# A hybrid decoder step on one core: meta rows and sequences in one chunk, the last input blocks between the chunks' steps, and one convolution tap on ScalarE

## The reference

```python
h = h + W_out(concat[GDN(xn), Conformer(xn)])      # xn = RMSNorm(h), one projection W_in for both
h = h + PEER(RMSNorm(h))                           # 128*128 experts of one neuron, 8 heads, top 16
y = RMSNorm(h)
# GDN: 4 heads of 128; q, k, v through a causal convolution of 4 taps and silu, q and k normalised
#   per chunk: decay = exp(G_i - G_j), L = strict(k beta k^T decay), solve (I + L) u = [v beta, k beta exp(G)]
#   v_new = u_v - w_k S;  o = (q exp(G)) S + (q k^T decay) v_new
#   S = S exp(G_last) + (k exp(G_last - G))^T v_new
#   prompt: one chunk of 16 meta rows, then chunks of 64; sequences: the recurrence, 4 steps each
# Conformer: glu = a * sigmoid(b); causal convolution of 31 taps over 512 channels; LayerNorm; silu
```

## Time and profile before

| | |
|---|---|
| median of 3 runs (us) | 1945.18 |
| lowest and highest (us) | 1933.81, 1945.46 |
| the profiled execution's own time (us) | 1947.19 |
| its span, first to last instruction (us) | 1945.5 |
| mean granted TensorE clock in it | 0.963 |

### The profile page before, as it was taken

The page is one execution under the profiler, slowest core; times in us unless marked ns, Lnnn a source line. Parts: engine busy times, 40 slices in busy tenths (PEclk is TensorE's granted clock), DMA queues, the critical chain, the costliest instruction groups (busy, mean ns, idle before and its releaser), DMA issues.

```text
span 1945.5 us, 29596 instructions
## 1 busy us (share of the span) xinstructions
PE 1819.2 (94%) x11654; PEld 1761.5 (91%) x11654; DVE 1432.6 (74%) x2619; ACT 659.0 (34%) x1046; POOL 668.3 (34%) x431
## 2 busy tenths in 40 slices
PE   5999676887989999999999999999999999999998
PEld 4999566765989999999999999999999999999997
DVE  4798788556359999999986666635878877888753
ACT  4444211112143334434343333333333333333332
POOL 2000000000000067767787676773324333333100
PEclk9999798875989999999999999999999999999999
DMA  7321100000552148798989999899999999999831
GB/s 192 88 66 53 50 1 1 1 1 19 163 168 85 45 153 280 257 310 286 324 295 311 301 312 313 304 318 374 350 356 384 356 348 341 367 341 339 326 122 36
DMA packets 190859, 424.86 MB, mean 218 GB/s; under 512 B 11188, under 2 KB 119248, under 8 KB 180473
## 3 DMA queue, kind: packets, MB, share of 16 engines
q1 hardware_dynamic: 153409, 287.99, 42.9%
q0 software_dynamic: 37312, 134.97, 19.5%
HBM read 361.28 MB, written 62.06 MB: 218 GB/s over the span
## 4 chain that ended last, share of the span: by engine, by line
PE 73%; DVE 22%; issue 2%; ACT 1%; DMA 1%; POOL 1%; SPq 0%; DVEq 0%; ACTq 0%; POOLq 0%
PE psum L1160 30%; PE psum L1139 20%; PE psum L829 9%; PE psum L1127 3%; PE psum L824 3%; PE psum L917 2%; DVE junk L2047 2%; DVE cT L1624 2%; DVE besti L1910 1%; DVE sring L1914 1%; DVE besti L1922 1%; PE psum L975 1%; DVE best L1918 1%; DVE best L1906 1%; DVE WR L1541 1%
## 5 line engine op out<-in xcount | busy, mean ns | idle before, releaser
L1139 PE MATMUL psum<-xT,WS 128*128 128x416 f32 x3072 | 594.7, 353 | 2.9 <-POOL WS L766 2.9
L1160 PE MATMUL psum<-AR,WS 128*128 128x416 f32 x3072 | 582.1, 351 | 2.6 <-DVE AR L2118 2.6
L1160 PEld LDWEIGHTS psum<-AR,WS 128*128 128x128 f32 x3072 | 575.6, 188 | 9.1 <-DVE AR L2118 3.0
L1139 PEld LDWEIGHTS psum<-xT,WS 128*128 128x128 f32 x3072 | 572.1, 188 | 8.5 <-POOL WS L766 4.1
L766 POOL TENSOR_TENSOR WS<-RAWP,WS 128x1024 fp32r<-128x1024 f32 x128 | 311.7, 2445 | 773.5 <-ACT WS L1441 673.0
L757 POOL DMA_INDIRECT rowg<-in_expert_v,idx x128 | 176.9, 1382 | 322.6 <-DVE acc L2061 315.1
L829 PE MATMUL psum<-xT,WR 128*128 128x280 f32 (+1 forms) x1968 | 261.1, 295 | 2.6 <-DVE xT L1567 2.6
L829 PEld LDWEIGHTS psum<-xT,WR 128*128 128x128 f32 x1968 | 258.2, 193 | 3.3 <-DVE xT L1567 3.2
L1451 ACT ACTIVATE WS<-RAWP 128x1024 fp32r<-128x1024 f32 x128 | 135.6, 1059 | 337.8 <-PE psum L1160 337.8
L2111 DVE TENSOR_TENSOR WS<-RAWP,WS 128x1024 fp32r<-128x1024 f32 x128 | 156.4, 1222 | 116.7 <-ACT WS L1451 116.7
L1478 ACT ACTIVATE actA<-psum 128x416 f32<-128x416 f32 x128 | 66.4, 519 | 402.9 <-PE psum L1139 402.7
(11 more groups left out here) (334 smaller groups left out, 1668.0 us busy)
## 6 DMA issues: line engine op xcount, KB each, us to landing
RAWP<-in_expert_u SPq DMA_DIRECT2D x64, 1024.0 KB, 6.3
RAWP<-in_expert_v SPq DMA_DIRECT2D x64, 1024.0 KB, 8.6
act_dram<-actA SPq DMA_DIRECT2D x128, 208.0 KB, 4.4
gate_dram<-gblk SPq DMA_DIRECT2D x26, 1024.0 KB, 10.5
act<-act_dram SPq DMA_DIRECT2D x64, 416.0 KB, 8.2
Gt<-gate_dram SPq DMA_DIRECT2D x16, 1664.0 KB, 9.7
RAW<-in_w_in SPq DMA_DIRECT2D x8, 1024.0 KB, 5.6
RAW<-in_w_query SPq DMA_DIRECT2D x8, 1024.0 KB, 5.6
```

What stands on the lines that cost most here:

```text
L1139: last = mm(bank[e % 2][:, 0:TD], ws(e)[:, pw, kt * P:(kt + 1) * P], xT[:, px, kt, TSP:TPE], start=(kt == 0 and i == 0), stop=(kt == KT - ...
L1160: last = mm(bank[dt][:, 0:TD], ws(NK + e)[:, pw, dt * P:(dt + 1) * P], AR[:, e % 4, pa, :], start=(e == 0 and i == 0), stop=(e == NK - 1 a ...
```

## The change

The 32 rows of the sequences and the 16 meta rows become one chunk of 48, chunk 0, and stand first in the rows, so that five chunks are left. Masks (`tri_m`, `neg_m`, `pos_m`) keep the sequences apart. The input blocks are put in the order ab, glu 0, qkv, glu 1, glu 3, glu 2, z 0, z 1. The last five of them (from `LATE`) are no longer a stretch of their own: their units, cut in halves of 12 products, are steps of the same written order as the chunks' steps. That order is now given by a level for each step. The sets of tiles are three. Each group of products waits for the readers of its bank's last group, in a ring of four banks while input blocks run, of six after. Exponentials get their bias on ScalarE, per head; the scalings of k and v and the decay of the state move from VectorE to ScalarE, per head; the copies of the tail rows too. The factor of q is left to the output's norm. The LayerNorm is computed with channels on partitions, its sums by products with ones. The sequences' states are updated within the stretch. The sums of q's and k's squares move to the last four qkv blocks, and the wait for `qk2` stays ahead of the interleaved part. The first tap of each qkv convolution is done by ScalarE after the unit is taken out. SyncE's loads (states, `h`, the rows of the norm, weights with other slots) are reordered accordingly.

```diff
-CHUNKS = [(0, 128), (128, 128), (256, 128), (384, 128), (512, 16), (TP, TS)]
-SAMPLE = len(CHUNKS) - 1
+MIXED = TS + META
+CHUNKS = [(0, MIXED)] + [(MIXED + P * i, P) for i in range(SEQ // P)]
...
-    blocks += [glu[1], z[0], z[1], glu[3], glu[2]]
+    blocks += [glu[1], glu[3], glu[2], z[0], z[1]]
...
+LATE = 8
...
+        SET = {0: 0, 1: 0, 2: 0, 3: 1, 4: 2}
+        FIRST = {0: 4.2, 1: 13.5, 2: 30.5, 3: 40.3, 4: 43.3}
+
+        LEVEL = {"k": 0, "gb": 0.1, "khT": 1, "kk": 2, "kq": 2.1, "ldT": 3, "v": 3.1, "p2": 4, "pt2": 4.1,
+                 "t1": 5, "p4": 5.1, "pt4": 5.2, "t2": 6, "p8": 6.1, "t3": 7, "n": 8, "nt": 8.1, "r0a": 8.2,
+                 "r0b": 8.3, "n2": 9, "r1a": 9.1, "r1b": 9.2, "nt2": 9.3, "nt4": 10, "r2a": 10.1, "r2b": 10.2,
+                 "r3a": 11, "r3b": 11.1, "wT": 12, "ws": 13, "qs": 13.1, "su": 14, "o1": 14.1}
...
+        SAMPLE_AT = {"sw0": 46.4, "sw1": 47.4, "sw2": 48.4, "sw3": 49.4, "sw": 49.5, "ws": 50.4, "qs": 50.5,
+                     "o1": 51.4}
...
+                  "onb": {SAMPLE: 52.7, 1: 53.7, 2: 54.7, 3: 55.7, 4: 58.2},
+                  "on": {SAMPLE: 53.2, 1: 54.2, 2: 55.1, 3: 56.2, 4: 59}}
+        NORM_AT = {"ls": 53.3, "lc": 53.35, "lv0": 54.3, "lv1": 54.8, "lv2": 55.25, "lv3": 55.8, "lr": 56.3,
+                   "lm": 56.8, "ln": 57.1}
+        MIX_AT = {"conformer": 57.4, "delta": 57.6}
+        TAILS_AT = {"tail0": 40.65, "tail1": 40.85, "tail2": 41.05, "tail3": 41.2}
+
...
+        EARLY_RING, RING = [4, 5, 6, 7], [4, 5, 6, 7, 0, 1]
+        LINEAR_END = 2 * (UNIT0[first["out"]] - UNIT0[LATE])
+
+        GBANK, BEFORE, held, ring = {}, {}, {}, {}
+        for n, ci, by in GROUPS:
+            r = EARLY_RING if turn(n, ci)[0] < LINEAR_END else RING
+            b_ = r[ring.get(len(r), 0) % len(r)]
+            ring[len(r)] = ring.get(len(r), 0) + 1
+            GBANK[n, ci], BEFORE[n, ci] = b_, held.get(b_)
+            held[b_] = [(e, m, ci) for e, m in by]
...
+            def late_blocks():
+
+                for b in range(LATE, first["out"]):
+                    for u in range(UNIT0[b], UNIT0[b + 1]):
+                        for half in range(2):
+                            yield ("lin", 2 * (u - UNIT0[LATE]) + half), LIN
+                            if half == 0 and u == UNIT0[b]:
+                                V.wait(pe, "low", b)
+                            unit_half(b, u, half)
...
+            for b in range(LATE):
                 linear(b)
                 scalars(b)
             V.wait(pe, "cum")
             V.wait(pe, "ab")
             V.wait(pe, "qk2")
...
+                        fn(qext[:, e, QC - 1 + cut:QEXT], src, ACT.Copy)
+                        fn(qtail[:, c, TS:], bk[:, HALF - (QC - 1):HALF], ACT.Copy, "unit", u)
+                        A.now(act)
+                        fn(qkv_of(c)[:, TS:], qext[:, e, 0:TP], ACT.Identity, "tap", c, scale=cols[:, c:c + 1])
...
+                        yield ("lin", 2 * k + 1), LIN
+                        evacuate_unit(b, u)
+                        if k == 0:
+                            V.wait(act, "qk2")
+                            fn(tok[:, RQ], tok[:, RQ], ACT.Sqrt)
+                            fn(tok[:, RK], tok[:, RK], ACT.Sqrt, "rqk")
+                        if k == 1:
+                            silu(2 * HEADS + 2)
+                            silu(2 * HEADS + 3)
+                        if u == UNIT0[b + 1] - 1 and b + 2 < first["out"]:
...
+                each_head(None, lambda hh: RA[0:c, hh, 1, :], of_head("k"), lambda hh: row_of(RKB, c, ci, hh), ci)
+                each_head("ke", lambda hh: KE[0:c, hh, :], of_head("k"), lambda hh: row_of(RKE, c, ci, hh), ci)
...
+                for hh in range(HEADS):
+                    fn(M[6][0:c, hh, 0:c], M[6][0:c, hh, 0:c], ACT.Exp, bias=row_of(GCB, c, ci, hh), scale=-1.0)
+                    fn(M[5][0:c, hh, 0:c], M[5][0:c, hh, 0:c], ACT.Exp, "exp", ci, bias=row_of(NGC, c, ci, hh),
+                       scale=1.0)
...
+            def row_scales():
+
+                T.wait(dve, "qk2", 2 * HEADS - 1)
+                for i, lo in ((RQ, 0), (RK, HEADS)):
+                    op(dve.tensor_scalar(tok[0:MIXED, i, 0, :], bank[7][0:MIXED, lo:lo + HEADS], EPS, None, ALU.add))
+                    op(dve.tensor_scalar(tok[:, i, LAST4], of_chunks(bank[7], lo), EPS, None, ALU.add), "qk2")
+                A.wait(dve, "rqk")
...
-                            if j == 0:
-                                chain(dve.tensor_scalar(d, x[:, j:j + TP], w, None, ALU.mult))
...
+                    A.wait(dve, "tap", c)
+                    for j in range(1, QC):
+                        w = cols[:, NQ * j + c:NQ * j + c + 1]
+                        chain(dve.scalar_tensor_tensor(d, x[:, j:j + TP], w, d, ALU.mult, ALU.add))
...
+                    if b == LATE:
+                        yield ("lin", k + 1.1), LIN
+                        row_scales()
+                    if b + 1 < first["out"] and b > LATE:
+                        yield ("lin", k + 1.2), LIN
+                        low(b + 1)
+                    if BLOCKS[b][0] == "glu":
+                        yield ("lin", k + 8.5), LIN
+                        glu(b)
...
-                yield "k"
-                chain(tt(KH[0:c], src("k", P), rows(RK, c, ci, P), ALU.mult), "k", ci)
-                op(tt(KE[0:c], KH[0:c], rows(EL, c, ci, P), ALU.mult), "KE", ci)
-                op(tt(RA[0:c, :, 1, :], KH[0:c], rows(BEG, c, ci, P), ALU.mult))
-                yield "v"
-                op(tt(RA[0:c, :, 0, :], src("v", P), rows(BETA, c, ci, P), ALU.mult), "v", ci)
-                V.counts["RA", ci] = V.n
-                yield "gb"
-                chain(tt(sq_(M[7]), src("gb"), rows(GC, c, ci, c), ALU.subtract), "gb", ci)
-                op(tt(sq_(M[6]), sq_(M[7]), mask(pos_s if s_ else pos), ALU.add))
-                op(tt(sq_(M[5]), sq_(M[7]), mask(neg_s if s_ else neg), ALU.add), "arg", ci)
-                yield "kk"
+                yield "k", ci
+                op(tt(KH[0:c], src("k", P), rows(RK, c, ci, P), ALU.mult), "k", ci)
+                yield "gb", ci
+                op(tt(sq_(M[6]), src("gb"), mask(pos if ci else pos_m), ALU.add))
+                op(tt(sq_(M[5]), src("gb"), mask(neg if ci else neg_m), ALU.add), "arg", ci)
+                yield "kk", ci
                 A.wait(dve, "exp", ci)
-                L = M[3] if c == P else M[0]
-                chain(tt(sq_(L), src("kk"), sq_(M[6]), ALU.mult), "kk", ci)
-                chain(tt(sq_(L), sq_(L), rows(BETA, c, ci, c), ALU.mult), "Ld", ci)
-                if c == P:
-                    chain(tt(sq_(M[0]), sq_(L), mask(diag16), ALU.mult), "Ld", ci)
-                    op(tt(sq_(M[7]), sq_(L), sq_(M[0]), ALU.subtract), "Lo", ci)
-                yield "kq"
-                op(tt(AT[0:c, :, 0:c], src("kq"), sq_(M[5]), ALU.mult), "kq", ci)
-                yield "ldT"
+                if ci:
+                    chain(tt(sq_(M[3]), src("kk"), sq_(M[6]), ALU.mult), "kk", ci)
+                    chain(tt(sq_(M[0]), sq_(M[3]), mask(diag16), ALU.mult), "Ld", ci)
+                    op(tt(sq_(M[7]), sq_(M[3]), sq_(M[0]), ALU.subtract), "Lo", ci)
+                else:
+                    op(tt(sq_(M[0]), src("kk"), sq_(M[6]), ALU.mult), "kk", ci)
+                    V.counts["Ld", ci] = V.n
+                yield "kq", ci
...
+            def feed():
+
+                if pieces[0] < CC * gated[0]:
+                    conv_to(pieces[0] + 1)
+
+            side_by_side([tile(ci) for ci in range(len(CHUNKS))]
+                         + [sample_tile(), norm_tile_conf(), mix_tile(), outs(), roots(), inverse_roots(),
+                            late_blocks()], feed)
+            low(first["out"])
```

1425 lines of the change are left out of this document (787 added, 638 removed).

## The result

The changed kernel takes 1923.78 us (median of 4 runs, 1917.61 to 1926.53) against 1945.32 (4 runs, 1933.81 to 1946.43): a ratio of 0.9893, 95% interval 0.9852 to 0.9933. The interval ends short of 1, so the kernel is faster, if by little. The forecast was 1869, the range 1838 to 1908: the sign was right and the size was off by 55 us.

The account below looks back on a forecast made before the run. A chunk's chain, not an engine, bounds the chunks' stretch. Mixed stretch 151.8 + 263 = 415, plus output stretch 71.8 starts queries at 486.8, 75.8 earlier: 1947.2 - 75.8 = 1871.4, median 2.0 lower, 1869; range 1838 to 1908.

Parts of the forecast that it names:

- What bounds the stretch: In the chunks' stretch, 223 to 477 us, a chunk's chain of products and readers bounds, not an engine.
- First tap, 0: Qkv convolutions: moving the first tap to ScalarE is worth 0 to 2 us, taken as 0.
- Up to the last block, 139.6: Input blocks: last qkv block ends at 133.0, three of four groups of sums of squares at 139.6, the fourth at 141.8.
- The new gap, ten us: Before the first late block TensorE waits for `qk2`, ten us idle, and resumes at 151.8.
- TensorE's sum, 213 at full clock: TensorE's work from 151.8 to the output projection: 213 us at full clock.
- VectorE's sum, 210: VectorE's work in the mixed stretch: 210 us, a full chunk falling from 38 operations of 512 elements to 26.
- How well the two overlap: Mixed stretch of TensorE and VectorE, added level by level: 263 us, an overlap of 81%, ending at 415.
- The clock's rival: Mixed stretch at clock 0.55: 213 becomes 387, time 1993, slower than before; decides from mean clock 0.62; chance 0.03.
- ScalarE's part: Mixed stretch: ScalarE busy about 120 of 260 us, not the bound, but its operations lie on the chain.
- Output stretch 71.8: Output projection to first query product: 71.8 us instead of 79.65, without the states' updates and the wait for `h`.
- the one in which the queues hold one another: Mixed stretch: waits for bank readers, taps and fixed half units give 70% overlap, 304 us, time 1910; chance 0.19.
- It isn't what it says: Chunks' stretch: third set of tiles could be worth nothing; whole change ends within 1%, chance 0.03.

Follow-up runs that it names:

- Closing both: Changed kernel with the last column sums read right after the last qkv convolution and TensorE waiting only at their bank's first use: stretch 306.9 us against 320.0.
- the two edits of order: Changed kernel with column sums read early and transposed keys copied ahead of the exponentials: 1899.53 us, ratio 0.9771 to the kernel before.
- the keys first: Changed kernel with ScalarE copying a chunk's transposed keys before its exponentials, the first product's four exponentials ahead of the others: stretch 299.6 us against 320.0.
- three chunks and the orders: Changed kernel with blocks first, three chunks in flight, both order edits, norm and weight splitting earlier: 1876.99 us, ratio 0.9650 to the kernel before.

## Why the prediction was wrong

- **What bounds the stretch**: right. No engine does; the chain does. Every run that took work out got back less than half of it (27.6 of 69, 21.5 of 46, 43.9 of 115, with the work as the expectations count it).
- **First tap, 0**: right: 12 taps changed engine, at 0.73 us instead of 0.49, and nothing came of it.
- **Up to the last block, 139.6**: 144.4, 4.8 us later. Every block was given 12.4 us, as from 108.24 on in the earlier trace rows. Three of them now stand behind column sums, and such a block takes 14.1 to 14.6, at a mean clock of 0.94 over the stretch. The kernel before shows it too, at 174.57 and 190.83, though not at 159.89 (12.60); first the changed kernel, then the kernel before:

```profile
127.99 2.39 PE L935 MATMUL psum<-ones,sqb 128*48 128x1 f32 x20
130.24 14.12 PE L892 MATMUL psum<-xT,WR 128*128 128x280 f32 x96
```

```profile
174.57 14.16 PE L829 MATMUL psum<-xT,WR 128*128 128x280 f32 x96
```

- **The new gap, ten us**: right, 10.21, and the wait for the roots after it (8.42, forecast "some 5"). Closing both was worth 13 us.
- **TensorE's sum, 213 at full clock**: the sum right, the clock wrong. At 0.87 the same products took 244.5: **31.5 us, the largest error of the prediction**, and the first half of the step that failed. The clock was weighed only as a rival that decides at 0.62, and stood in the sum as nothing, though the earlier trace rows had 0.82 for the chunks and the earlier trace rows 1.00 for a part of them only.
- **VectorE's sum, 210**: 199 measured. ScalarE's, 120: 131, with 20 table loads between 35 and 467 us where the kernel before had 15.
- **How well the two overlap**: here the prediction failed. It had 263 us, an overlap of 81%, and 309.8 came. The step is that a level got TensorE's work at full clock and little more than the larger of two engines' sums. By levels (the forecast's idle time is its length less TensorE's sum in it):

| levels | forecast | measured | idle, forecast | idle, measured | busy, at clock |
|---|---|---|---|---|---|
| half units only | 7 | 8.7 | 0 | 0 | 8.7 at 0.69 |
| chunk 0 | 30 | 34.5 | 5 | 5.9 | 28.6 at 0.85 |
| chunk 1 and the level after | 62 | 75.1 | 8 | 15.3 | 59.8 at 0.93 |
| chunk 2's first ten | 37 | 37.6 | 3 | 2.9 | 34.7 at 1.00 |
| the rest with the tail | 127 | 153.9 | 32 | 41.2 | 112.7 at 0.82 |

  The clock makes 31.5 of the 46.8 us, some 20 of them in the last row, and more idle time than the forecast's 50 makes 15.3, about 7 of them with chunk 1 and 9 in the last row (the parts of the forecast hold 215 us of TensorE's and not 213, so their idle time adds up to 48). The larger engine's sum came out for chunk 2 (37.6), which was alone in flight with only taps on VectorE between its steps. It failed for chunk 1, alone too, which had two glu and two `low` of VectorE's besides and a sigmoid with its table ahead of its copy; and it failed with two and three chunks in flight. So the number of chunks in flight doesn't tell where the rule holds. That a level costs the sum of what the chain meets on its way, the copy behind exponentials and table, the reader behind a tap or a glu, fits chunk 1 and the two edits of order, but no run tests it level by level. That the low clock follows from the same waits is likely and not shown: it rose to 0.90 and 0.91 with the keys first, but with three chunks and the orders it was 0.93 in one run and 0.89 in another with the same idle time.
- **Slips in its working**: the parts that it names for VectorE in chunk 1 (23 pairs of 1.45, three more, two glu, two `low`) add up to 49 and not 53, which makes the miss there larger. The clock's rival reads 1947 + 48 = 1993; it is the median, 1945, to which 48 is added. And the sentence that the trace agrees with that rival at 430 us doesn't hold as told: TensorE stood still for only 0.5 of those 20 us at 0.54, so the low clock there isn't one of waits within them.
- **ScalarE's part**: "it isn't the bound, but its operations lie on the chain" stood there, and no price did. One edit of its order took 20.5 us off in one run. Its table loads cost what the row says: 1.28 from 204.56, the exponentials at 205.85. The Trainium skill, ScalarE: Activation LUTs, section What ACT_TABLE_LOAD costs, adds a drain of 1.38 us to each; the trace has none, so the measurement decides.
- **Output stretch 71.8**: 72.4, and `h` hidden, right. The stretch after it: 2.9 us longer, taken as 0.
- **The rivals**: the one in which the queues hold one another gave 304 for the stretch and 1910 for the time; with 309.8, 4.8 for the late start and 2.9 at the end, that is the case whose number came. Its reason was right in the taps and the half units (together 43.9 of the stretch by leaving them out) and wrong in the ring. That 70% fitted is in part luck: TensorE was busy for 79% of the stretch, and it is the clock, which this rival didn't price, that brings the 213 at full clock down to 69%. "It isn't what it says" was partly true: with three sets, the third chunk came into flight only at 330, and chunks in flight from the start of the chunks' part, with the blocks apart, gave 23.8 us. By the Trainium skill, TensorE: Matmul & The Clock Gate, section HAM oscillation, waits between bursts cost the clock as well. The trace agrees here, with 0.69 in the 8.70 us behind the gap, 0.82 in 312.8 to 466.7, where TensorE is busy for 73%, and 1.00 in 275.2 to 312.8, where it is for 92%. It doesn't agree everywhere: in the earlier trace rows TensorE is busy for 78% at 1.00 and for 98% at 0.54.

Left open: why the stretch after the queries is 2.9 us longer, what each of the waits costs through the clock, and what the third set of tiles alone is worth in the changed kernel's own order, which wasn't tried.
